# Two transformer blocks on one core: own PSUM banks in attention, later decay rows, and a tile, a norm and a projection pair in halves of 256 tokens

## The reference, cut to what matters

```python
# first block (attention branch): 8 heads of 64, two key/value groups
yn = _nsa(q_raw, q_rope, kc, vc, ks, vs, kw, vw, gates)
merged = sigmoid(g_a) * (ya @ w_branch_a) + sigmoid(g_b) * ((yn * silu(n_z)) @ w_branch_b)
x = _rmsnorm(x + merged @ w_out, final_norm_g)
...
# second block: first feed-forward part, then the norm and the mixer's projections
h = modulate(rms_norm(x, norm_g[0]), shift[0], scale[0])
x = x + 0.5 * gate[0] * swiglu(h, ffn1_w_in, ffn1_w_out)
h = modulate(rms_norm(x, norm_g[1]), shift[1], scale[1])
proj = h @ mix_w_in          # xp, q, k, v, z, b_raw, a_raw, g_pool, g_dn
...
# gated delta rule, chunks of 64 tokens, 8 heads of 128
gc = cumsum(g)
decay = exp(where(causal, gc[i] - gc[j], -inf))
kk = einsum('nbhik,nbhjk->nbhij', kc, kc)
a_mat = where(strict, beta * kk * decay, 0)
sol = triangular_solve(a_mat + eye, rhs)
```

## Time and profile before

| | |
|---|---|
| median of 3 runs | 1939.75 us (1938.55 to 1940.95) |
| the profiled execution | 1941.54 us, its span 1939.9 us |
| busy share: PE, PEld, DVE, ACT, POOL | 98%, 81%, 52%, 39%, 10% |
| chain that ended last: PE, DVE, ACT, DMA | 91%, 4%, 2%, 1% |
| mean granted clock of TensorE | 0.995 |

### The profile page before, as it was taken

How to read it: one execution, slowest core, us unless ns; L and a number is a source line. 1 busy time by engine, 2 the same in 40 slices (tenths; PEclk the granted TensorE clock), 3 DMA queues, 4 the chain that set the end, 5 groups by cost and what they waited for, 6 DMA issues and landing times.

```text
span 1939.9 us, 25741 instructions
## 1 busy us (share of the span) xinstructions
PE 1901.1 (98%) x9472; PEld 1576.7 (81%) x9472; DVE 1004.2 (52%) x1414; ACT 756.6 (39%) x1437; POOL 193.9 (10%) x242
## 2 busy tenths in 40 slices
PE   6999999999999999999998999999999999999998
PEld 5888878777788888888887788899888888888887
DVE  5687566566576563333335666454643573333332
ACT  4445534365433442222223654343422342222332
POOL 1101010000010000000011245044000100000010
PEclk9999999999999999999998999999999999999999
DMA  8767513211286323333333233211324333333331
GB/s 309 253 179 207 187 35 101 66 34 50 76 253 208 99 87 98 97 97 92 104 93 104 77 88 99 60 38 45 97 85 148 98 88 96 99 96 95 100 99 55
DMA packets 330904, 212.90 MB, mean 110 GB/s; under 512 B 21373, under 2 KB 315450, under 8 KB 330302
## 3 DMA queue, kind: packets, MB, share of 16 engines
q1 hardware_dynamic: 319830, 170.27, 30.4%
q0 software_dynamic: 10368, 37.75, 5.8%
q10 hardware_dynamic: 616, 3.67, 0.5%
HBM read 204.31 MB, written 7.35 MB: 109 GB/s over the span
## 4 chain that ended last, share of the span: by engine, by line
PE 91%; DVE 4%; ACT 2%; DMA 1%; issue 1%; SPq 1%; POOL 0%; DVEq 0%; ACTq 0%
PE psum L437 25%; PE psum L439 25%; PE psum L438 25%; PE psum L1513 2%; PE psum L1032 1%; PE psum L1034 1%; PE psum L1033 1%; PE psum L1304 1%; PE psum L1317 1%; DMA late_ada_w<-in_ada_w 1%; DVE delta_qkv_T L2279 1%; PE psum L1202 1%; PE psum L1218 1%; PE psum L1403 1%; PE psum L1336 1%
## 5 line engine op out<-in xcount | busy, mean ns | idle before, releaser
L437 PE MATMUL psum<-act_hi,w_hi 128*128 128x512 f32 x1616 | 648.2, 401 | 2.9 <-DVE act_lo L2279 2.5
L439 PE MATMUL psum<-act_hi,w_lo 128*128 128x512 f32 x1616 | 631.5, 391 | 0.0
L438 PE MATMUL psum<-act_lo,w_hi 128*128 128x512 f32 x1616 | 631.2, 391 | 0.0
L396 DVE TENSOR_TENSOR w_lo<-w_raw,w_hi 128x1024 fp32r<-128x1024 f32 x306 | 382.9, 1254 | 338.3 <-ACT w_hi L388 317.2
L388 ACT ACTIVATE w_hi<-w_raw 128x1024 fp32r<-128x1024 f32 x306 | 319.7, 1052 | 181.8 <-PE psum L439 173.4
L437 PEld LDWEIGHTS psum<-act_hi,w_hi 128*128 128x128 f32 x1616 | 304.6, 189 | 67.6 <-issue 6.9
L439 PEld LDWEIGHTS psum<-act_hi,w_lo 128*128 128x128 f32 x1616 | 304.3, 188 | 64.9
L438 PEld LDWEIGHTS psum<-act_lo,w_hi 128*128 128x128 f32 x1616 | 304.8, 189 | 60.7 <-issue 1.4
L437 PE MATMUL psum<-ffn_hi,w_hi 128*128 128x512 f32 (+1 forms) x374 | 141.7, 379 | 0.0
L439 PE MATMUL psum<-ffn_hi,w_lo 128*128 128x512 f32 (+1 forms) x374 | 140.9, 377 | 0.0
L438 PE MATMUL psum<-ffn_lo,w_hi 128*128 128x512 f32 (+1 forms) x374 | 140.9, 377 | 0.0
(11 more groups left out here) (375 smaller groups left out, 2376.5 us busy)
## 6 DMA issues: line engine op xcount, KB each, us to landing
w_raw<-in_ffn_w_in SPq DMA_DIRECT2D x88, 512.0 KB, 3.7
w_raw<-in_w_in SPq DMA_DIRECT2D x68, 512.0 KB, 3.8
w_raw<-in_mix_w_in SPq DMA_DIRECT2D x52, 512.0 KB, 3.7
ada_w<-in_ada_w POOLq DMA_DIRECT2D x48, 512.0 KB, 4.9
w_raw<-in_ffn_w_out SPq DMA_DIRECT2D x32, 512.0 KB, 4.1
late_ada_w<-in_ada_w POOLq DMA_DIRECT2D x24, 512.0 KB, 4.8
w_raw<-in_ffn_w_out SPq DMA_DIRECT2D x16, 384.0 KB, 3.3
w_raw<-in_w_branch_a SPq DMA_DIRECT2D x8, 512.0 KB, 5.0
```

The source lines that it names most:

```text
L396: dve.tensor_tensor(WLO[:, n % 4, :], RAW[:, n % 4, :], WHI[:, n % 4, :].bitcast(F32), ALU.subtract).then_inc(w_lo, 1)
L437: pe.matmul(out, whi, hhi, start=start, stop=False)
L438: pe.matmul(out, whi, hlo, start=False, stop=False)
L439: return pe.matmul(out, wlo, hhi, start=False, stop=stop)
```

## The change

Four things change.

**Attention's banks.** In step 0 the four score products go to banks 4, 5, 6 and 7. Only step 0's second pair used to wait for banks 3 and 0; now it waits for the compressed branch's probabilities, and step 1's second pair waits for banks 3 and 0. Transposes go to the bank of the unit's own scores (4 for units 0 and 1 of a step, or 4, 5 and 3 in steps 8 to 15), the last transfer of a step to bank 6. In steps 0 to 7 both pieces of oz stand together ahead of both transfers (oz(2)) instead of one ahead of each. A score product that writes into a bank with transposes waits until they are copied.

**Halves of 256 tokens.** The last output tile of ffn1_out, the norm behind it and first_pair run for tokens 0 to 255 and then for 256 to 511. The second half of the tile has bank 7, and the sums and spread of the first half stand in it after its 4th and 10th input chunk; those of the second half stand in the first half of the pair, after normed tiles 2 and 5. half_mean and half_diagonal are the mean, reciprocal and diagonal of two of the four columns, half_square and half_root the square and root of a half, half_hi and half_lo the high and low part of a normed half tile. The coefficients coef(1) of this norm are made before the residuals, and the split of small2's second and third weight chunk moves behind them: ScalarE's and VectorE's split of chunk 1 stands behind half_root(0) and half_diagonal(0), that of the next one behind the first half's normed tiles. Steps between the engines are counted by a semaphore half_step.

**Decay rows.** decay_sums and the eight decay_rows stand half a tile of k2 later (first in the middle of tile 5 instead of behind tile 4), and VectorE's masks are spread over three tiles instead of two.

**The pool's second quarter** stands directly behind the first, ahead of the transposes that wait for the inverse, instead of behind them. GpSimd's two semaphores for its constants become one.

```diff
-        RAW_AT, H_AT, AHEAD_OF = {1: 8, 3: 32}, {1: 16, 2: 24, 3: 40}, {1: "ffn1_in", 3: "ffn2_in"}
+        RAW_AT, H_AT, AHEAD_OF = {1: 8, 3: 40}, {1: 16, 2: 24, 3: 48}, {1: "ffn1_in", 3: "ffn2_in"}
         SHIFT_OF, COEF_OF = {1: MOD, 3: MOD + 48}, {1: FCOEF, 3: COEF}
+        half_step = sem("first_half_tile_to_spread")
+        HALF_STEP = {n: k + 1 for k, n in enumerate(("done", "x", "square", "sum", "mean", "root", "diagonal", "spread"))}
+        NORMED_AT = {1: NT, 2: NT + 8, 3: NT + 24}
...
-            return 4 if u == 63 else 6
+            return 6 if u % 4 >= (2 if u < 32 else 3) else SCORE_BANK[u % 4]
+        def score_bank(u):
+            return (4, 5, 6, 7)[u] if u < 4 else SCORE_BANK[u % 4]
...
+            def half_sums(half):
+                pe.wait_ge(sem("squares_added"), 6)
+                if half:
+                    pe.wait_ge(half_step, HALF_STEP["mean"])
+                    pe.wait_ge(sem("squares_ready"), NT + 16)
+                else:
+                    pe.wait_ge(half_step, HALF_STEP["square"])
+                for part, slot in enumerate((0, square_slot(2, KD - 1))):
+                    for n in (2 * half, 2 * half + 1):
+                        mm = pe.matmul(PS[:, 4, n:n + 1], SQ[:, slot, n * P:n * P + P], ONES[:, 0:1],
+                                       start=(part == 0 and n == 2 * half), stop=(part == 1 and n == 2 * half + 1))
+                    if half:
+                        mm.then_inc(sem("square_sum"), 1)
+                if not half:
+                    mm.then_inc(half_step, 1)
+            def half_spread(half):
+                if half:
+                    pe.wait_ge(sem("rms_diagonal"), 2)
+                else:
+                    pe.wait_ge(half_step, HALF_STEP["diagonal"])
+                for n in range(2):
+                    mm = pe.matmul(PS[:, 5 + half, n * P:n * P + P], ONES, RDIAG[:, 2 * half + n, :], start=True, stop=True)
+                mm.then_inc(sem("rms_spread") if half else half_step, 1)
+            def halved_tile(pl, f):
+                for half in range(2):
+                    tok = half_tok(half)
+                    bank = PS[:, 7, tok] if half else pe_open(pe, pl, f)[:, tok]
+                    for c, (k0, kn) in enumerate(((0, 8), (8, 8), (16, 6))):
+                        n = pl.chunk + 3 * f + c
+                        pe.wait_ge(w_lo, n + 1)
+                        for kk in range(kn):
+                            a = slice(kk * P, kk * P + P)
+                            mm = mm3(pe, bank, WHI[:, n % 4, a], WLO[:, n % 4, a], HIDHI[:, k0 + kk, tok],
+                                     HIDLO[:, k0 + kk, tok], c == 0 and kk == 0, c == 2 and kk == kn - 1)
+                            if half and kk == kn - 1:
+                                mm.then_inc(chunk_done, 1)
+                            if half and (c, kk) == (0, 3):
+                                half_sums(0)
+                            elif half and (c, kk) == (1, 1):
+                                half_spread(0)
+                    if not half:
+                        mm.then_inc(half_step, 1)
+            def halved_pair(tiles, base):
+                banks = [pe_open(pe, pl, t) for pl, t in tiles]
+                pe.wait_ge(w_lo, tiles[1][0].chunk + tiles[1][1] + 1)
+                for half in range(2):
+                    tok = half_tok(half)
+                    for kk in range(KD):
+                        pe.wait_ge(h_ready, base + 8 * half + kk + 1)
+                        for bank, (pl, t) in zip(banks, tiles):
+                            n, a = pl.chunk + t, slice(kk * P, kk * P + P)
+                            mm = mm3(pe, bank[:, tok], WHI[:, n % 4, a], WLO[:, n % 4, a], HHI[:, kk, tok], HLO[:, kk, tok],
+                                     kk == 0, kk == KD - 1)
+                            if half and kk == KD - 1:
+                                mm.then_inc(chunk_done, 1)
+                        if not half and kk == 1:
+                            half_sums(1)
+                        elif not half and kk == 4:
+                            half_spread(1)
...
-                    for f in range(8 if name == "ffn1_out" else 7):
+                    for f in range(7):
...
+                    if name == "ffn1_out":
+                        halved_tile(pl, 7)
...
                 if p % 2 == 0 and p:
                     pe.wait_ge(sem("exp_done"), 2 * p)
+                    pe.wait_ge(sem("pt_ready"), turned_by(2 * p - 3))
+                elif p > 17:
+                    pe.wait_ge(sem("pt_ready"), turned_by(2 * p - 4))
                 elif p == 1:
+                    pe.wait_ge(sem("cmp_pt_ready"), 4)
+                elif p == 3:
                     pe.wait_ge(bank_free[3], (Place("oz1", 0).tile + 14) // 4 + 1)
                     pe.wait_ge(bank_free[0], (Place("oz1", 0).tile + 15) // 4 + 1)
...
-                if us[0] == 0:
-                    pe.wait_ge(sem("cmp_pt_ready"), 2)
-                elif turn_bank(us[0]) == 6:
-                    pe.wait_ge(sem("pt_ready"), turned_by(us[0]) - 1)
+                if us[0] >= 4 and turn_bank(us[0]) == 6:
+                    pe.wait_ge(sem("pt_ready"), turned_by(us[0] // 4 * 4) - 1)
...
+                        mm = pe.transpose(PS[:, turn_bank(us[0]), k * n + j:k * n + j + P], PR[u % 4][:, j:j + P], ID)
...
+                if q < 8:
+                    oz(2)
                 for us in turns(q):
-                    if us != (63,):
+                    if q >= 8 and us != (63,):
                         oz(1)
...
-            rms_sum(2)
-            rms_spread(2)
-            first_pair([(Place("small2", 0), 0), (Place("k2", 0), 0)], H_AT[2])
+            halved_pair([(Place("small2", 0), 0), (Place("k2", 0), 0)], H_AT[2])
...
                 if t in (5, 6):
-                    decay_rows(4 * t - 18)
-                    decay_rows(4 * t - 17)
+                    if t == 5:
+                        decay_sums()
+                    decay_rows(4 * t - 20)
+                    decay_rows(4 * t - 19)
...
-                elif t in (4, 5):
-                    if t == 4:
-                        decay_sums()
-                    decay_rows(4 * t - 16)
-                    decay_rows(4 * t - 15)
+                elif t in (5, 6):
+                    decay_rows(4 * t - 18)
+                    decay_rows(4 * t - 17)
...
                     quarter(Place("pool2", 0), 0, 0)
+                    quarter(Place("pool2", 0), 0, 1)
...
-                    quarter(Place("pool2", 0), 0, 1)
...
+            half_square(0)
+            half_root(0)
+            split_hi(act, Place("small2", 0), 1)
+            for k in range(4):
+                half_hi(0, k)
+            half_square(1)
+            for k in (4, 5):
+                half_hi(0, k)
+            half_root(1)
+            for k in (6, 7):
+                half_hi(0, k)
             split_hi(act, Place("small2", 0), AHEAD)
+            for k in range(KD):
+                half_hi(1, k)
...
+            coef(1)
             residual("ffn1_out", 3, MOD + 16, normed=True)
-            coef(1)
-            rms(2, COEF, MOD + 24)
+            def half_residual(half):
+                pl, f = Place("ffn1_out", 0), KD - 1
+                dve.wait_ge(chunk_done, pl.chunk + 24) if half else dve.wait_ge(half_step, HALF_STEP["done"])
+                tok = half_tok(half)
+                chained(stt(XT[:, f, tok], PS[:, 7 if half else pl.bank(f), tok], col(MOD + 16 + f), XT[:, f, tok],
+                            ALU.mult, ALU.add))
+                if half:
+                    dve.sem_inc(x_ready, 1)
+                else:
+                    dve.sem_inc(half_step, 1)
+                    dve.sem_inc(bank_free[pl.bank(f)], 1)
...
+            def half_lo(half, k):
+                tok = half_tok(half)
+                dve.wait_ge(sem("h_hi"), H_AT[2] + 8 * half + k + 1)
+                stt(HLO[:, k, tok], SQ[:, k % 4, tok], col(MOD + 24 + k), HHI[:, k, tok].bitcast(F32), ALU.add, ALU.subtract)\
+                    .then_inc(h_ready, 1)
+            def half_normed(half, k):
+                tok = half_tok(half)
+                if k == 0:
+                    dve.wait_ge(sem("rms_spread"), 2) if half else dve.wait_ge(half_step, HALF_STEP["spread"])
+                if k >= 4:
+                    dve.wait_ge(h_ready, H_AT[2] + 8 * half + k - 3)
+                stt(SQ[:, k % 4, tok], XT[:, k, tok], col(COEF + k), PS[:, 5 + half, 0:256], ALU.mult, ALU.mult)\
+                    .then_inc(sem("normed"), 1)
+                if k:
+                    half_lo(half, k - 1)
+            half_residual(0)
+            half_mean(0)
+            half_diagonal(0)
+            split_lo(dve, Place("small2", 0), 1)
+            for k in range(4):
+                half_normed(0, k)
+            half_residual(1)
+            for k in (4, 5):
+                half_normed(0, k)
+            half_mean(1)
+            half_normed(0, 6)
```

(48 more changed lines are left out.)

22 lines of the change are left out of this document (11 added, 11 removed).

## The result

The changed kernel takes 1930.72 us, median of 6 runs (1929.77 to 1931.30), against 1940.35 us of the kernel before in the runs beside it: ratio 0.9949, 95% interval 0.9938 to 0.9959, that is 8 to 12 us less. Forecast were 1930.0 and 9.7 us less. The profiled execution has a span of 1929.5 us, 10.4 less than before; with 1931.30 us it is the slowest of the six.

What follows compares the result with a forecast made beforehand. TensorE, busy for 98% of the span, was taken as the bound. Gains of 1.8 (attention), 4.4, 2.6 and 0.9 sum to 9.7 us, taking the median 1939.75 to 1930.0; own range 1927.5 to 1932.0, chance 0.58.

Steps and rivals of the forecast that it cites:

- Step 0: Attention's first step: 1.7 us less if the clock stays up; fall taken as happening, gain 0.2, bounds 0 and 1.7.
- Steps 1 to 7: Attention: next scores wait for ScalarE's copy, 0.4 lost in four steps, 0.4 gained in step 4; loss 1.2 us.
- Steps 8 to 15: Attention: each of four transposes gets its own bank, so waits for the copy out of bank 6 go; gain 2.8 us.
- Tile, norm, pair: Last output tile, norm and first pair in halves: gain 4.4 us, bounds 2.1 and 5.6, with a new 1.9 wait.
- the rival of 0.49 apart: Norm and first pair: VectorE's small operations lie 0.49 us apart, 2.3 us more, 1932.3 in all; chance 0.12.
- the slower rival: Tile and pair: weight loads, 0.19 long, set the pace of 256-column matmuls; kernel would take 1946 us; chance 0.03.
- the 4.7: Tile, norm and pair: the pair's end moves from 1060.2 to 1055.5, 4.7 us earlier, before small costs make it 4.4.
- Decay rows: Decay rows half a tile later: stalls of 3.6 us go, one wait of 1.0 stays; gain 2.6, bounds 1.5 and 3.6.
- Pool's quarter: Pool's second quarter ahead of the transposes fills the wait for the inverse: gain 0.9 us, bounds 0.5 and 1.1.
- The clock in the pair: Rival: the clock falls in the first pair's new wait, price 1.6 us, time 1931.6; chance 0.14.

Runs made afterwards that it cites:

- third gate piece: Changed kernel with a third gate piece in step 0, taken from step 14, and one ahead of each transfer in steps 1 to 7: 1926.90 us, ratio 0.9926.

## Why the prediction was right

The mechanism was right in all four parts, and all terms but step 0's came within 0.4 us. That the total is right to 0.1 us (9.6 between the medians, 9.7 forecast) is in part luck: in the profiled execution step 0 gave 1.5 more than forecast, and two stretches outside the sum took 1.4 back.

- *Step 0*: "I take the fall as happening: gain 0.2, bounds 0 and 1.7." This is the mis-sized term. The upper bound and the term itself were both measured in the same code: without the fall the gain is 1.7; with it steps 0 and 1 take 14.5 against 14.26, which is 0.1 gained in step 0 once the 0.36 that step 1 loses anyway is set apart. The price of a low stretch (1.5) was right at 1.6. What failed was to treat a chance as a yes or no: a term that depends on the clock at a wait near the one that lowered it has two values, each with a share of the executions.
- *Steps 1 to 7*: loss 1.2 forecast, 1.05 measured, with the waits of 0.35 and the copies as described: steps 1, 2, 5 and 6 lose 0.36 to 0.39 each, step 4 gains 0.40. Steps 3 and 7 ended with VectorE's scaling and changed by less than 0.05, as said.
- *Steps 8 to 15*: gain 2.8 forecast, 3.0 measured.
- *Tile, norm, pair*: 4.4 forecast, 4.8 measured. Measured from the tile's first matmul at 1020.85, the pair's first half ends at 1045.1 (24.3 later; forecast 24.4), TensorE goes on 25.7 later (forecast 26.3 with a wait of 1.9; it was 1.5 with what the list leaves out) and the pair ends 32.0 later (forecast 32.4). VectorE's first low part of the second half was ready 25.7 after the tile's start, 0.4 earlier than I had added up. Its operations lie 0.40 apart, as taken, though each is drawn 0.48; the rival of 0.49 apart is refuted. The 256-column matmuls keep their pace of 0.12, and the weight loads, 0.19 long in the drawing, don't set it: the slower rival is refuted too.
- *The old cost of the norm*: the terms listed behind the 4.7 don't add up to it: 1.5 + 2.5 + 0.8 of waits and 2.4 of slow matmuls, less 1.5 and 1.9, is 3.8. What is missing is that the clock had fallen earlier than the earlier trace rows shows, at 1041.5, still in the wait for the diagonal, so that the spread ran at half clock too:

```profile
1042.35 2.07 PE L901 MATMUL psum<-rms_diagonal,constants 128*128 128x128 f32 x8 [1.51 <-DVE rms_diagonal L2276]
```

```profile
1041.00:1042.00 1.00, 0.00 (x0) 0.00 (x0) 0.69 (x3) 0.24 (x2) 1.00 (x2) 0.77 0.99 410
1042.00:1044.00 2.00, 1.65 (x7) 1.65 (x8) 0.29 (x1) 0.00 (x0) 0.70 (x2) 0.50 1.15 451
```

  The same eight matmuls take 1.06 at full clock (at 683.93 in the same profile), 1.0 less.
- The formula that the Trainium skill (VectorE: DVE Perf Modes, section on the TRN2 errata) gives for an fp32 tensor_tensor, taken for these operations, makes an estimated 0.42 for 256 columns and 0.69 for 512. The spacings measured are 0.40 and 0.65, so the formula is near the spacing of queued operations, not their drawn length. Its warning about small tiles holds as a price, 60% of the time for half the columns, and the edit pays it on an engine that has room, except in the pair's second half. That the formula would make the term 1.5 us better than mine, as the prediction says, has no working and doesn't follow: the sum used a spacing of 0.40, already below 0.42. The 0.4 by which the term came out larger doesn't speak for it.
- *Decay rows*: 2.6 forecast, 2.2 measured: the one wait for mask 2 is 0.9 with its hidden part (1.0 forecast), and the second pair of rows starts 0.74 behind its transposes where 0.43 was seen before.
- *Pool's quarter*: 0.9 forecast, 1.0 measured.
- *Outside the sum*: the start cost 0.4 and the output projection 1.0 in the profiled execution. Neither belongs to the change: the start takes 369.1 to 372.2 us in the thirteen profiles with one code, and the kernel with only the rows and the quarter changed has the wait of the output projection too. In the profiled execution they cancel most of what step 0 gave more than forecast; 1.8 + 4.4 + 2.6 + 0.9 = 9.7 stands against 3.7 + 4.8 + 2.2 + 1.0 = 11.7, less 1.4.
- *The clock in the pair*: the rival did not come about. Ten profiles have the halves; the clock is 1.00 in the pair in all of them, eight with the wait of 1.3 and two without. One reason given against this rival was wrong, though: of the "waits of 1.0 and 1.5 us elsewhere" that left the clock up, the one of 1.5 is the wait for the diagonal shown above, in which it fell. The one of 1.0 (before the transposes at 428.62) did leave it up.

Left open: what decides in a single execution whether the clock falls behind the wait of 2.26, and how often it does (three of six profiles is all there is); and with it how much of step 0's 1.7 is in the median of the changed kernel.

## What to carry to other kernels

When an edit moves an engine's wait, ask what that engine could do in it: the halves gained because the norm's chain lay beside matmuls, a third gate piece filled the one in step 0, and the weight split behind the normed tiles and the masks ahead of a split are its counterpart: work that isn't urgent is taken out from in front of work that is. A filler belongs between a transfer into a bank and the next write to that bank, so that the copy is covered. And a gain of 1 us in a kernel of 1930 can't be seen in its median; cut the timelines at the same instructions and compare the stretch.

## What the runs showed of the hardware

Whether the granted clock falls at an idle stretch of TensorE was not decided by the length of the wait alone. With waits in step 0 of 0.90 us the clock stayed at 2.4 GHz (2 of 2 profiles), with 2.26 it fell to 1.2 GHz in 3 of 6, with 2.79 in 4 of 4, with 3.62 in the one there is. That looks like an order by length, but how much work stood ahead of the wait differs too (three gate pieces, two, none, one). And elsewhere shorter waits were enough: behind 1.06 us in the output projection it fell in both profiles that have it, while behind 1.30 us in the pair it stayed up in 8 of 8. Near the start, where the code is that of all thirteen kernels, it fell in twelve profiles and stayed up in one (the third gate piece), with a wait of 2.38 us there as in the changed kernel, in which it fell.

Nor did the fall always come at one place. TensorE took up work at 377.41 and the clock was still 1.00 until 379; with the wait of 2.79 us (before the change) it fell at 375.9, 0.85 us after TensorE had gone on; with 3.62 us it fell in the wait, at 375.1, while TensorE went on at 375.89. The low stretch was 3.4 us long after all waits up to 2.79 us in step 0 and 6.8 us after the longest, and 10.2 us in the old norm with its waits of 0.78, 1.51 and 2.47 us.

The Trainium skill (TensorE: Matmul & The Clock Gate, part 1 on the clock gate) says that how many matmuls run at the low clock differs from run to run of the same kernel at its start. These profiles agree for the start, twelve against one, and show the like in the middle of a kernel: three against three. It also says that the clock has only two levels; the windows at 0.73 and 0.56 are consistent with a change of level inside them.
